# A two-layer diffusion backbone: bias in one fp32 pass, modulation pieces moved, mixers in a new order, products on GpSimd

## What is computed

```python
def swiglu(h, w13, w2):
    g, u = jnp.split(h @ w13, 2, axis=-1)
    return (jax.nn.silu(g) * u) @ w2

# one sub-layer of each layer, x = [context 256; latent 256], width 1024
h = modulate(rms_norm(x, norm), shift, scale)      # h * (1 + scale) + shift
x = x + 0.5 * gate * swiglu(h, w13, w2)            # D_FF = 2816; mixer: x + gate * (mixer(h) @ w_out)
# shift, scale, gate: 3 of 9 chunks of c @ w_mod + b_mod   (w_mod: 1024 x 9216 a layer)

# the mixer: three groups of heads read p = h @ w_in
# A: 4 heads of differential attention; B: 4 heads of windowed attention with a sink
# C: a bidirectional state-space scan, 8 heads, chunks of 128 tokens
decay_in = jnp.exp(segsum(a))                      # a = dt * A, per head, lower triangle
cb = jnp.einsum('bclgn,bcsgn->bcgls', cc, bc)
y_diag = jnp.einsum('bcgls,bcgrls,bcsgrp->bclgrp', cb, decay_in, xdt)
```

## Time and profile before

| | us |
|---|---|
| median of 3 runs | 1889.11 (1888.89 to 1890.87) |
| profiled execution | 1888.78 |
| its span | 1887.1 |
| PE, DVE, ACT, POOL busy | 1811.9, 1423.3, 752.0, 51.6 |
| mean granted clock | 0.968 |

### The profile page before, as it was taken

One profiled execution on the slowest core, in us unless ns is written; L12 is line 12 of the kernel. 1 busy time (PEld: TensorE's weight loads), 2 busy tenths in 40 slices (PEclk: granted clock), 3 DMA queues, 4 the chain that ended last, 5 costly groups with the idle time before them and its releaser, 6 DMA issues.

```text
span 1887.1 us, 26111 instructions
## 1 busy us (share of the span) xinstructions
PE 1811.9 (96%) x9314; PEld 1496.1 (79%) x9314; DVE 1423.3 (75%) x2351; ACT 752.0 (40%) x1147; POOL 51.6 (3%) x101
## 2 busy tenths in 40 slices
PE   8999999997999899899999999999999799899999
PEld 5788888886776577688888888888888578589999
DVE  5887877788877767887777678777786888756665
ACT  4322222246656656222222372222224654754342
POOL 1000000000000000000000000000000000000000
PEclk8899999998998899899999999999999899979999
DMA  8444444422312033534444423444440332134543
GB/s 352 179 151 183 147 159 168 182 80 93 119 45 90 1 134 116 197 133 178 155 156 161 151 75 148 159 168 162 156 156 29 114 111 88 48 112 178 180 178 110
DMA packets 37585, 259.47 MB, mean 137 GB/s; under 512 B 4369, under 2 KB 5841, under 8 KB 7441
## 3 DMA queue, kind: packets, MB, share of 16 engines
q1 hardware_dynamic: 26066, 182.32, 26.5%
q0 software_dynamic: 11456, 76.32, 11.0%
HBM read 252.60 MB, written 5.24 MB: 137 GB/s over the span
## 4 chain that ended last, share of the span: by engine, by line
PE 84%; DVE 6%; ACT 6%; issue 3%; DMA 1%; POOL 0%; ACTq 0%; DVEq 0%; POOLq 0%
PE ps L1514 25%; PE ps L1515 25%; PE ps L1516 25%; PE ps L1622 1%; DVE mod_prod L951 1%; ACT w_hi L546 1%; ACT n_t L598 1%; PE ps L1830 1%; DMA scale_w<-scale_in 1%; PE ps L1772 1%; PE ps L1891 1%; PE ps L1795 1%; DVE x_res L1056 1%; PE ps L1805 1%; PE ps L1645 1%
## 5 line engine op out<-in xcount | busy, mean ns | idle before, releaser
L1514 PE MATMUL ps<-h_hi,w_hi 128*128 128x512 f32 (+1 forms) x1840 | 680.3, 370 | 26.3 <-DVE w_lo L933 10.4
L1515 PE MATMUL ps<-h_lo,w_hi 128*128 128x512 f32 (+1 forms) x1840 | 673.7, 366 | 0.0
L1516 PE MATMUL ps<-h_hi,w_lo 128*128 128x512 f32 (+1 forms) x1840 | 672.9, 366 | 0.0
L1514 PEld LDWEIGHTS ps<-h_hi,w_hi 128*128 128x128 f32 x1840 | 350.5, 190 | 90.7 <-issue 22.9
L1516 PEld LDWEIGHTS ps<-h_hi,w_lo 128*128 128x128 f32 x1840 | 350.2, 190 | 57.4
L1515 PEld LDWEIGHTS ps<-h_lo,w_hi 128*128 128x128 f32 x1840 | 350.6, 191 | 56.6 <-issue 1.2
L928 DVE TENSOR_TENSOR w_lo<-raw,w_hi 128x2048 fp32r<-128x2048 f32 x132 | 301.9, 2287 | 82.3 <-ACT w_hi L546 82.2
L1056 DVE SCALAR_TENSOR_TENSOR x_res<-ps,abg,x_res 128x256 f32<-128x256 f32 x584 | 248.4, 477 | 151.2 <-PE ps L1516 150.2
L546 ACT ACTIVATE w_hi<-raw 128x2048 fp32r<-128x2048 f32 x132 | 252.2, 1911 | 268.0 <-PE ps L1516 268.0
L951 DVE CUSTOM_DVE_ANT_0 mod_prod<-mod_raw,cb 128x1024 f32<-128x1024 f32 x256 | 301.5, 1218 | 2.6 <-ACT cb L738 2.5
L1514 PE MATMUL ps<-a_hi,w_hi 128*128 128x512 f32 (+1 forms) x640 | 235.5, 368 | 16.1 <-DVE x_res L1056 12.5
(11 more groups left out here) (231 smaller groups left out, 1594.9 us busy)
## 6 DMA issues: line engine op xcount, KB each, us to landing
raw<-ffn_in SPq DMA_DIRECT2D x132, 1024.0 KB, 4.8
mod_raw<-mod_in POOLq DMA_DIRECT2D x68, 1024.0 KB, 5.0
raw<-proj_in SPq DMA_DIRECT2D x20, 1024.0 KB, 4.9
raw<-out_w_in SPq DMA_DIRECT2D x8, 1024.0 KB, 4.7
x_spill<-x_res SPq DMA_DIRECT2D x2, 2048.0 KB, 7.2
x_res<-x_spill SPq DMA_DIRECT2D x2, 2048.0 KB, 7.9
scale_w<-scale_in POOLq DMA_DIRECT2D x4, 512.0 KB, 13.1
x_res<-x_in SPq DMA_DIRECT2D x2, 1024.0 KB, 11.3
```

The source lines that it names most:

```text
L1514: pe.matmul(dst, w_hi[:, slot, wsl], hi, start=first, stop=False)
L1515: pe.matmul(dst, w_hi[:, slot, wsl], lo, start=False, stop=False)
L1516: return pe.matmul(dst, w_lo[:, slot, wsl], hi, start=False, stop=last)
```

## The change

Six things are changed.

1. The bias is formed of the fp32 weights in `raw` by the fp32 shift in abg, 16 fp32 matmuls of 2 columns instead of 32 fp32r ones of 4 columns. It stands at the beginning of the first unit, behind a wait for bank 4 to be read (`evac`). shift_r and its split go; DVE's reduction becomes a copy. SP waits for the bias before it loads over that slot. In f=3 the mean goes from k=2 to k=5.
2. f=0 forms 1.5 pieces in each of turns 1 to 4, one in turns 5 to 9 and the last (pieces 4 to 15); f=1 forms none at its start.
3. In the mixers t = x times root is done by POOL, h_lo stays on DVE; the norm's tiles (n.0 to n.8), first_scaled (e.0), derive (dv.0) and the layer's vectors (la.0) are tokens of WEAVE now.
4. The 16 mask products hm of each layer are done by POOL, in order behind the rows' copies (128x512 in layer 0, 128x256 in layer 1).
5. The decay rows are five parts instead of four.
6. Both lists of WEAVE are new; most tiles are projected in halves.

```diff
-        MOD_PRE = {0: (2, 2), 1: (14, 2)}
+        MOD_PRE = {0: (2, 2)}
-        STRETCH = {0: [(1, PAIRS - 1, 4)], 1: [(1, PAIRS - 1, 16)], 2: [(1, PAIRS - 1, 25)], 3: [(1, PAIRS - 1, None)]}
-        LAST_PIECE = {0: 13}
+        STRETCH = {0: [(1, 5, 4), (5, PAIRS - 1, 10)], 1: [(1, PAIRS - 1, 16)], 2: [(1, PAIRS - 1, 25)], 3: [(1, PAIRS - 1, None)]}
+        LAST_PIECE = {0: 15}
...
-                "cv.0 E.0 E.1 S.0 T0.0 T.2 E.2 R.0 R.1 R.2 E.3 cv.1 T.3 T.4 cv.2 S.1 R.3 E.4 E.5 si.0 cv.3 S.2 si.1 si.2 si.3 "
+                "dv.0 n.0 n.1 n.2 n.3 T0.0 T.2 Ta.4 n.4 n.5 e.0 la.0 S.-1 E.0 E.1 Tb.4 Ta.5 n.6 n.7 Tb.5 n.8 cv.0 E.2 R.0 R.1 E.3 "
...
+            def mixer_norm(n):
+                pool.wait_ge(acc_done, 7 * n + 7)
+                pool.wait_ge(rstd_done, 2 * n + 2)
+                for d in range(KT):
+                    if d >= 2:
+                        pool.wait_ge(h_lo_s, 8 * n + d - 1)
+                    pool.tensor_tensor(n_t[:, d % 2, :], x_res[:, d, :], n_rstd[:, :], ALU.mult).then_inc(t_done, 1)
+            def masked_decay(layer, i):
+                nt = out_tokens(layer)
+                m = m_t[:, i % RING, 0:nt]
+                pool.wait_ge(ex_done, DECAYS * layer + i + 1)
+                pool.tensor_tensor(m, m, cbt[:, i // 8, 0:nt // P, :].rearrange("p c t -> p (c t)"), ALU.mult).then_inc(mt_done, 1)
...
+                def turn(i, tiles):
+                    middle = 1 + len(tiles) // 2
+                    down(i - 1, base + 3 * i + 1, tiles=tiles[:2], gate_split=(2, f, i))
                     split(0, f, i + 1)
+                    for tile in tiles[2:middle]:
+                        mod_tile(*tile)
                     dve.wait_ge(unit_done, base + 3 * i + 2)
                     product(f, i, nt, a_hi, a_lo)
                     split(1, f, i + 1)
+                    for tile in tiles[middle:]:
+                        mod_tile(*tile)
...
-            def unit_bias(n, slot):
-                pe.wait_ge(shift_done, 2 * n)
+            def unit_bias(n):
+                pe.wait_ge(derive_s, DERIVED_AB[n])
                 for m in range(2):
                     for k in range(KT):
-                        wsl = slice(256 * k + P * m, 256 * k + P * m + P)
-                        pe.matmul(ps[:, BIAS_AT, 4 * m:4 * m + 4], w_hi[:, slot, wsl], shift_r[:, k, :], start=(k == 0), stop=False)
-                        last = pe.matmul(ps[:, BIAS_AT, 4 * m:4 * m + 4], w_lo[:, slot, wsl], shift_r[:, k, :], start=False, stop=(k == KT - 1))
+                        last = pe.matmul(ps[:, BIAS_AT, 2 * m:2 * m + 2], raw[:, 0, 256 * k + P * m:256 * k + P * m + P],
+                                         abg[:, n, 1, :, k], start=(k == 0), stop=(k == KT - 1))
                 last.then_inc(bias_mm, 1)
-            def first_unit(n, turn, nt, hi, lo, tile=None):
+            def first_unit(n, turn, nt, hi, lo, evac, tile=None):
                 split_ready(0, turn)
+                pe.wait_ge(*evac)
+                unit_bias(n)
                 for k in range(KT):
...
-                    if k == 2:
+                    if k == (2 if nt == T else 5):
                         mean(n, nt)
-                    elif k == 5:
-                        unit_bias(n, 0)
```

More of the change, by code:

```diff
@@ L415, in load_mix @@
                     sp.wait_ge(lo_ready, base - 2 if m == 0 else base - 1 if m == 1 else base + m - 1)
+                    if m == 2:
+                        sp.wait_ge(bias_mm, 3 * layer + 1)
                     if m == 3:
@@ L480, in load_stretches @@
                 for lo, hi, q0 in STRETCH[f]:
-                    if q0 is not None:
+                    if (f, lo) == (0, 1):
+                        with pool.Fori(0, 2) as t:
+                            for q in range(3):
+                                load_piece(3 * t + (q0 + q))
+                    elif q0 is not None:
                         with pool.Fori(lo, hi) as i:
@@ L508, in mixer_rows @@
                                    src.partition_broadcast(64)).then_inc(etb_in, 16)
+                for i in range(DECAYS):
+                    masked_decay(layer, i)
             load_half(0, 0)
@@ L582, in scaled_high, with norm_root @@
                 x.then_inc(u_hi_s, 1)
-            def norm_rest(n, nt, first_unit=None, after={}):
+            def norm_root(n, nt):
                 table_ln_exp()
@@ L680, in ffn_phase @@
                     else:
[L681 removed]
+                        norm_root(n, ntn)
             def mixer(layer):
@@ L693, in mixer @@
                     if kind == "E":
-                        if j >= 2:
+                        if j < 2:
+                            first_evacuation(layer, j)
+                        else:
                             evacuate(layer, j)
+                    elif kind == "n" and j < KT:
+                        norm_tile(3 * layer + 1, j, T, base)
                     elif kind == "S":
@@ L699, in mixer @@
                         decay_rows(layer, j)
-                        if layer == 0 and j == 3:
+                        if layer == 0 and j == 4:
                             act.wait_ge(masks_in_s, 16)
@@ L743, in first_evacuation @@
                 act.wait_ge(pads, layer + 1)
-                for j in range(2):
-                    act.wait_ge(scaled_s, 2 * n - 1 + j)
-                    for s in range(2):
-                        x = act.activation(xpad[:, j, s, 2:2 + LAT], ps[:, j, s * LAT:(s + 1) * LAT], ACT.Identity, bias=bias[:, j, s:s + 1])
-                    x.then_inc(pj_evac, 1)
+                act.wait_ge(scaled_s, 2 * n - 1 + j)
+                for s in range(2):
+                    x = act.activation(xpad[:, j, s, 2:2 + LAT], ps[:, j, s * LAT:(s + 1) * LAT], ACT.Identity, bias=bias[:, j, s:s + 1])
+                x.then_inc(pj_evac, 1)
             def evacuate(layer, g):
@@ L859, in decay_rows @@
                     act.activation(r[3], r[2], ACT.Ln).then_inc(row_act, 1)
-                elif part == 2:
+                elif part == 3:
                     act.wait_ge(row_dve, rd + 5)
@@ L1020, in first_scaled, with norm_tile @@
                     tt(ps[:, m, 0:nt], ps[:, m, 0:nt], n_rstd[:, 0:nt], ALU.mult).then_inc(scaled_s, 1)
-            def norm_rest(n, nt, after={}):
-                def remainder(d):
-                    dve.wait_ge(h_hi_s, 8 * n + d + 1)
-                    tt(h_lo[:, d, 0:nt], n_t[:, d % 2, 0:nt], h_hi[:, d, 0:nt], ALU.subtract).then_inc(h_lo_s, 1)
-                dve.wait_ge(acc_done, 7 * n + 7)
-                dve.wait_ge(rstd_done, 2 * n + 2)
-                for d in range(KT):
+            def norm_tile(n, d, nt):
+                if d == 0:
+                    dve.wait_ge(acc_done, 7 * n + 7)
+                    dve.wait_ge(rstd_done, 2 * n + 2)
+                if d < KT and n % 3 != 1:
                     if d >= 2:
@@ L1034, in norm_rest @@
                     tt(n_t[:, d % 2, 0:nt], x_res[:, d, 0:nt], n_rstd[:, 0:nt], ALU.mult).then_inc(t_done, 1)
-                    if d >= 1:
-                        remainder(d - 1)
+                if d >= 1:
+                    dve.wait_ge(h_hi_s, 8 * n + d)
+                    tt(h_lo[:, d - 1, 0:nt], n_t[:, (d - 1) % 2, 0:nt], h_hi[:, d - 1, 0:nt], ALU.subtract).then_inc(h_lo_s, 1)
+            def norm_rest(n, nt, after={}):
+                for d in range(KT + 1):
+                    norm_tile(n, d, nt)
                     if d in after:
                         after[d]()
-                remainder(KT - 1)
             def product(f, i, nt, hi, lo):
@@ L1087, in ffn_phase, with down @@
                 derive(n, "g")
-                def down(i, units, add_n=None, piece=None, gate_split=None):
+                if f == 1:
+                    dve.wait_ge(cb_ready, 6)
+                def down(i, units, add_n=None, tiles=(), gate_split=None):
                     for d in range(KT):
@@ L1099, in down @@
                             split(*gate_split)
-                        if piece is not None and d in (3, 7):
-                            mod_tile(piece, d // 4)
+                        if tiles and d in (3, 7):
+                            mod_tile(*tiles[d // 4])
                         if add_n is not None and d >= 2:
@@ L1114, in turn, with tiles_of @@
                     split(1, f, i + 1)
-                    if piece is not None:
-                        mod_tile(piece, 3)
+                    for tile in tiles[middle:]:
+                        mod_tile(*tile)
+                def tiles_of(piece):
+                    return [] if piece is None else [(piece, j) for j in range(4)]
                 def last_turn(piece):
@@ L1133, in ffn_phase @@
                 for lo, hi, q in STRETCH[f]:
-                    with dve.Fori(lo, hi) as i:
-                        turn(i, None if q is None else i + (q - lo))
+                    if (f, lo) == (0, 1):
+                        with dve.Fori(0, 2) as t:
```

(25 more changed lines are left out.)

100 lines of the change are left out of this document (41 added, 59 removed), and 67 rows, old and new, of the table WEAVE.

## The result

The changed kernel took 1908.89 us (median of 4, 1907.45 to 1909.78) against 1889.14: ratio 1.0102, interval 1.0084 to 1.0119. It is 20 us slower, outside the predicted range.

What follows compares the result with a forecast made beforehand. TensorE, busy 96% of the span, was taken as the bound, so time moves only where it idles or runs at lower clock. +0.3 + 4.5 - 9.7 + 5.2 + 5.5 + 0.5 - 2.0 = +4.3 on 1888.8: 1893 us, range 1880 to 1903.

Steps and rivals of the forecast that it cites:

- The work costs PE nothing more. The place does: Bias at five first units: 16 fp32 matmuls take 3.63 us against 3.6 before, but now stand ahead of the mean.
- 5.2 us of delay: Mean, root, norm tiles and evacuation behind the early bias come 5.2 us later: 3.6 of work, 1.6 of lower clock.
- +4.5, +5.2, +5.5, +0.5 at the beginnings: Added us at the starts of mixer 0, f=2, mixer 1 and f=3, in that order.
- 4.4 + 0.9: f=1's start: silu ends at 743.6 against PE's arrival at 739.2, costing 4.4 of wait and 0.9 of clock.
- the mixers' beginnings: Mixer 0's tiles end 4.5 us later (bounds -4, +8); mixer 1's second split holds PE 5.5 longer (bounds -3, +9).
- the rest of both mixers: Both mixers after their beginnings, in the new order: -2 us, bounds -13 and +8.
- signs of being wrong: Wrong if f=0's turns grow, clock stays up, silu isn't the second unit's wait, or tails change over 10 us.
- f=1's start: Moving the pieces away removes 15.0 us of idle and lower clock; the later silu takes some back, net -9.7.
- f=0: Turns 1 to 4 form six tiles instead of four, DVE 30.7 of 32.8 us: +0.3 in all, bounds 0 and +6.
- Rival D: Products on GpSimd hold up DVE, by a shared port lock: +8 us, 1901; chance 0.18.
- Rival B: The new order undoes what the five late means cost, tails giving 11 instead of 2: 1884; chance 0.28.
- Rival C: The late mean costs only its 3.6 us, without clock, 1.6 less at each of four beginnings: 1887; chance 0.14.

Runs made afterwards that it cites:

- b1: The kernel before with the modulation pieces alone moved (1.5 in four turns of f=0, none at f=1's start): 1872.56 us, ratio 0.9913.
- a2: The changed kernel with the mixers' norm products (t = x times root) on VectorE again: 1902.03 us, ratio 1.0064.
- b6: The kernel before with 16 fp32 bias matmuls in place of the 32 fp32r ones, behind k=5: 1902.42 us, ratio 1.0067.
- b2: The kernel before with the fp32 bias alone, placed ahead of the first unit: 1911.39 us, ratio 1.0133.
- b7: The kernel before with its own 32 fp32r bias matmuls placed ahead of the first unit: 1912.55 us, ratio 1.0123.
- d4: The kernel before with the 16 norm products of the mixers on GpSimd, nothing else: 1900.80 us, ratio 1.0058.

## Why the prediction was wrong

The medians between neighbours make the way from before to after: 1890.4, pieces -17.9, order and masks -5.7, fp32 form in place +7.9, norm on GpSimd +5.2, bias first +29.0, together +18.5 of the 19.7 measured. They hold for this way alone: the +7.9 belong to the bias in place, and the +29.0 take that cost away again and put the late chain there.

**Bias first, direction right, size wrong.** "The work costs PE nothing more. The place does" held, and so did the wait for silu at f=1 and f=2. Forecast were 5.2 us of delay, and +4.5, +5.2, +5.5, +0.5 at the beginnings, with 4.4 + 0.9 given back of f=1's gain. The delay is 6.8, since the clock behind the bias at the unit's start costs 2.6 and the pass 4.15. At f=2 it cost 7.3 against 5.2: I priced the silu and left out that the second unit waits for the same late tiles. At f=3 +0.5 was forecast and measured, but 0.0 and -3.0 both occur there with the same code (the kernel before and b1), so that term is not tested.

**The failed step is the mixers' beginnings.** I followed the chain to project 3 and one unit on, and got +4.5 and +5.5 for them and -2 for the rest of both mixers. By the 192nd projection product the mixers are 10.5 and 10.3 us later than before, counted from their own starts; the rest adds 3.7 and takes 1.9, +1.8 in all. So the two beginnings miss 10.8 us, two thirds of the 16.7 between 4.3 and 21.0.

At mixer 0 I let project 3 wait for the evacuation, 6.1 us later than before. It waits for w_lo (the row of 448.61 above, 3.93 us) and comes 9.2 later from the start. In the new order this split, S.-1, stands behind six norm tiles instead of three, so that it takes all of the late mean (6.8 instead of 5.2) and of GpSimd's pitch (1.98 instead of 1.85, and the first hand-over). With VectorE's products (a2) project 3 comes 7.0 later instead of 9.2. Behind the wait the clock is 0.50 from 449 to 454, 2.5 us that I had no term for. The wait of about 5 us that I expected in T.6's place came (4.90 at 475.86). At mixer 1 there are two waits for w_lo, 7.77 and 4.75 us, with a clock of 0.54 and 0.58 in the 7 us from 1503 and from 1524. Project 3 comes 13.1 us later from the mixer's start, where I had 10, and the second wait ends 10.0 later, where I had 5.5. The stretch at the lower clock behind the first wait had no term here either.

The wait of the loads for the bias was in no term of the sum either. It costs 7 us a mixer with the bias in place (b6), but in the changed kernel, with the bias first, it isn't part of the loss: b2 and b7 lose the same with and without it.

None of the prediction's signs of being wrong came true: f=0's turns kept their length, the clock fell, silu was what the second unit waits for, and no tail changed by 10 us. The list had no sign for a mixer's beginning.

**f=1's start** was forecast -9.7, measured -11.3, and -15.5 without the late chain (b1), the 15.0 of the earlier trace rows. **f=0** was forecast +0.3; DVE's busy time rose from 261.27 to 278.81 in 328 us, and from turn 1 to the end the turns took the same 16.32 us per 72 matmuls. VectorE was busy 0.87 to 0.92 of the second to fourth turn, a little less than the 0.93 forecast. What is there, 1.5 of 1.9, came before turn 1, and varies between executions of like kernels (-0.4 to 1.7).

**Rival D** (GpSimd against VectorE) is seen, but not as the price. A mask product began within a w_lo of VectorE (546.95 to 549.24) and took 2.37 us; two together take 2.56:

```profile
544.16 2.56 POOL L511 TENSOR_TENSOR m_t<-m_t,cbt 128x512 f32<-128x512 f32 x2 [10.25 <-ACT m_t L751]
548.04 2.37 POOL L511 TENSOR_TENSOR m_t<-m_t,cbt 128x512 f32<-128x512 f32 x1 [1.33 <-ACT m_t L751]
```

The lock in the Trainium skill (SBUF — State Buffer, SBUF: two separate sides) says so: whichever of the two starts first keeps the shared ports for the whole instruction. This trace agrees both ways, with 2.37 instead of 1.28 us for the product that began second here, and 1.06 instead of 0.69 for the h_lo of 436.14. But undoing all 32 mask products moved the time by 1 us. For a lone product the trace has 1.28 us, where I took 1.05 from two MEMSET passes. The 1.2 us worked out from the Trainium skill (GPSIMD Engine Reference, 3.1 Elementwise), an estimate, was nearer. **Rival B** (the new order) came true in part: up to 6 us, masks included, with the other edits undone. **Rival C** was false: the clock fell.

## What to carry to other kernels

Ahead of a reduction that a long chain waits for, nothing is free on the engine that makes it: 4 us of work of the same price, moved past one small matmul, cost 21 to 29 us. Before an operand is taken from a load buffer instead of a copy, look at who loads into that buffer next and who stands behind its reader. And an edit bundle is to be split before it is judged: here -18 and +29 stood in one change.

## What had not been expected of the hardware

- An unbroken row of 32 small matmuls, 3.6 to 4.2 us, brings the clock to 0.50 for 3 to 6 us when it opens the unit; the same matmuls in groups of four, between full ones, leave it at 1.00.
- GpSimd's fp32 product of 128x512 takes 1.28 us from three SBUF streams, 2.4 times its MEMSET (0.525).
- f=3's start is 3 to 4 us faster in b1 (-3.0) and d4 (-4.1) than in the kernel before, whose f=3 is the same. What decides was not tried.
- The same attention tail of mixer 0 took 127 us at a clock of 0.91 before and 135 at 0.86 in d4. What decides was not tried.
